# Transposing a unit's probabilities four steps behind its scores in place of three

## What is computed

```python
def hybrid_mixer(x, positions, w_in, conv_w, rel_bias, w_out):
    proj = jnp.einsum('bsd,dp->bsp', x, w_in)
    (cb, cc, ch, dq, dk, dv, iq, ik, iw, cq, ck, cv) = jnp.split(proj, offs, axis=-1)
    y_conv = short_conv_mixer(cb, cc, ch, conv_w)
    y_dsa = dsa_attention(dq, dk, dv, iq, ik, iw)
    y_chk = chunk_band_attention(cq, ck, cv, rel_bias)
    return jnp.einsum('bsm,md->bsd', jnp.concatenate([y_conv, y_dsa, y_chk], axis=-1), w_out)

def one_block(args):                                   # of dsa_attention
    logits = jnp.einsum('bqhd,bsd->bqhs', iqb, ik)
    score = jnp.einsum('bqh,bqhs->bqs', iwb, jax.nn.relu(logits))
    _, idx = lax.top_k(score, topk)                    # 128 keys of at most 512
    s = jnp.einsum('bqhd,bqkd->bhqk', qb, k_sel) * scale
    p = jax.nn.softmax(s, axis=-1)
    return jnp.einsum('bhqk,bqkd->bqhd', p, v_sel)
```

## Time and profile before

| | us |
|---|---|
| median of 3 executions | 2910.43 (2909.35 to 2912.76) |
| the profiled execution | 2910.82 |
| its span, first to last instruction | 2909.0 |
| PE busy | 2803.4 |
| DVE busy | 1659.9 |
| ACT busy | 1264.3 |
| POOL busy | 420.5 |

### The profile page before, as it was taken

How to read it: one execution, slowest core, us unless ns; L and a number is a source line. 1 busy time by engine, 2 the same in 40 slices (tenths; PEclk the granted TensorE clock), 3 DMA queues, 4 the chain that set the end, 5 groups by cost and what they waited for, 6 DMA issues and landing times.

```text
span 2909.0 us, 39181 instructions
## 1 busy us (share of the span) xinstructions
PE 2803.4 (96%) x15778; PEld 2360.8 (81%) x15782; DVE 1659.9 (57%) x2517; ACT 1264.3 (43%) x2157; POOL 420.5 (14%) x337
## 2 busy tenths in 40 slices
PE   8999999999989999999999999999999999999997
PEld 7878999998877788887668878888776688788886
DVE  5786545454776745445875466333659754563335
ACT  5574322234574422224554545333445535453333
POOL 2221000001222000001343120000313431200003
PEclk9999999999999999999999999999999999999999
DMA  4111232322112333232123213323221232233332
GB/s 143 50 44 66 88 95 83 96 91 80 52 44 66 98 99 95 97 98 84 52 76 113 87 66 95 99 94 98 84 80 55 71 111 88 72 95 94 95 98 69
DMA packets 71923, 244.36 MB, mean 84 GB/s; under 512 B 9152, under 2 KB 10816, under 8 KB 71744
## 3 DMA queue, kind: packets, MB, share of 16 engines
q1 hardware_dynamic: 66528, 235.50, 25.1%
q10 hardware_dynamic: 5216, 6.36, 0.7%
HBM read 239.73 MB, written 2.10 MB: 83 GB/s over the span
## 4 chain that ended last, share of the span: by engine, by line
PE 83%; DVE 11%; ACT 2%; issue 2%; POOL 1%; DMA 0%; ACTq 0%; DVEq 0%
PE psum L574 23%; PE psum L580 23%; PE psum L577 23%; PE psum L643 2%; DVE temp L2162 2%; DVE small L2160 1%; PE psum L669 1%; PE psum L675 1%; PE psum L671 1%; DVE weights_hi_lo L1723 1%; PE psum L1065 1%; PE psum L1077 1%; PE psum L762 1%; PE psum L904 1%; DVE small L2133 1%
## 5 line engine op out<-in xcount | busy, mean ns | idle before, releaser
L574 PE MATMUL psum<-act_hi_lo,weights_hi_lo 128*128 128x264 f32 (+2 forms) x2544 | 776.3, 344 | 3.6 <-ACT temp L1267 2.8
L577 PE MATMUL psum<-act_hi_lo,weights_hi_lo 128*128 128x264 f32 (+2 forms) x2544 | 752.5, 335 | 1.9 <-DVE weights_hi_lo L1723 1.9
L580 PE MATMUL psum<-act_hi_lo,weights_hi_lo 128*128 128x264 f32 (+2 forms) x2544 | 752.4, 335 | 0.0
L1160 ACT ACTIVATE weights_hi_lo<-weights_float 128x1024 fp32r<-128x1024 f32 (+2 forms) x446 | 463.6, 1042 | 524.6 <-PE psum L580 455.3
L1723 DVE TENSOR_TENSOR weights_hi_lo<-weights_float,weights_hi_lo 128x1024 fp32r<-128x1024 f32 (+2 forms) x446 | 555.4, 1246 | 224.1 <-ACT weights_hi_lo L1160 223.1
L574 PE MATMUL psum<-hidden_hi_lo,weights_hi_lo 128*128 128x512 f32 (+2 forms) x1584 | 520.7, 358 | 7.8 <-ACT arena L1503 4.8
L580 PE MATMUL psum<-hidden_hi_lo,weights_hi_lo 128*128 128x512 f32 (+2 forms) x1584 | 512.7, 353 | 2.3 <-POOL hidden_hi_lo L1986 2.2
L577 PE MATMUL psum<-hidden_hi_lo,weights_hi_lo 128*128 128x512 f32 (+2 forms) x1584 | 511.5, 353 | 0.0
L574 PEld LDWEIGHTS psum<-act_hi_lo,weights_hi_lo 128*128 128x128 f32 x2544 | 440.0, 189 | 70.8 <-issue 17.7
L577 PEld LDWEIGHTS psum<-act_hi_lo,weights_hi_lo 128*128 128x128 f32 x2544 | 439.3, 189 | 48.5 <-issue 2.6
L580 PEld LDWEIGHTS psum<-act_hi_lo,weights_hi_lo 128*128 128x128 f32 x2544 | 438.9, 189 | 48.2
(11 more groups left out here) (277 smaller groups left out, 3320.7 us busy)
## 6 DMA issues: line engine op xcount, KB each, us to landing
weights_float<-in_w_ff SPq DMA_DIRECT2D x128, 512.0 KB, 3.6
weights_float<-in_w_gu SPq DMA_DIRECT2D x88, 512.0 KB, 3.6
weights_float<-in_w_in SPq DMA_DIRECT2D x70, 512.0 KB, 3.7
weights_float<-in_w_down SPq DMA_DIRECT2D x32, 448.0 KB, 3.3
weights_float<-in_w_out SPq DMA_DIRECT2D x16, 512.0 KB, 3.6
weights_float<-in_w_down SPq DMA_DIRECT2D x16, 512.0 KB, 3.5
weights_float<-in_w_mv SPq DMA_DIRECT2D x16, 512.0 KB, 3.2
weights_float<-in_w_mix SPq DMA_DIRECT2D x16, 512.0 KB, 3.3
```

Source lines behind the costliest of these rows:

```text
L574: e.matmul(slot[:, place:place + c1 - c0], w_hi[:, col], x_hi[:, c0:c1], start=first, stop=False)
L577: e.matmul(slot[:, place:place + c1 - c0], w_lo[:, col], x_hi[:, c0:c1], start=False, stop=False)
L580: mm = e.matmul(slot[:, place:place + c1 - c0], w_hi[:, col], x_lo[:, c0:c1], start=False, stop=final)
L1160: e.activation(K.parts(n)[0][:, 0:cols], K.staged(n)[:, 0:cols], ACT.Copy).then_inc(*K.did("hi", n))
```

## The change

The transposes of a unit move from step t+3 to t+4, the weighted sums from t+4 to t+5, and with them ACT's two copies; DVE's low half moves from t+5 to t+6. Scores, exponentials, sums of probabilities and POOL's scaling stay where they were. The numbers of instructions stay the same on every engine.

```diff
--- before.py
+++ after.py
@@ -912,16 +912,16 @@
                 B.emptied((4 + c,), ("exp2", l, u, c))
 
     def turn(s):
-        if s - 3 in UNIT_AT2:
-            u, kind, p, i = UNIT_AT2[s - 3]
+        if s - 4 in UNIT_AT2:
+            u, kind, p, i = UNIT_AT2[s - 4]
             for c in range(2):
                 B.clear(6 + c)
                 w.wait_ge(*done("scaled", l, u, c))
                 for j in range(i + 1):
                     mm = e.transpose(K.bank[6 + c][:, j * P:(j + 1) * P], K.probs2[u % 2][c][:, j * P:(j + 1) * P], ident)
                 mm.then_inc(*did("turned2", l, u, c))
-        if s - 4 in UNIT_AT2:
-            u, kind, p, i = UNIT_AT2[s - 4]
+        if s - 5 in UNIT_AT2:
+            u, kind, p, i = UNIT_AT2[s - 5]
             w.wait_ge(*done("tok", l, 3))
             for c in range(2):
                 w.wait_ge(*done("turned2_out", l, u, c))
@@ -2098,8 +2098,8 @@
     for p in range(4):
         split_lo(e, w, K, first + p + 3)
     for s in range(TOK_STEPS, STEPS2 + 2):
-        if s - 5 in UNIT_AT2:
-            u, kind, p, i = UNIT_AT2[s - 5]
+        if s - 6 in UNIT_AT2:
+            u, kind, p, i = UNIT_AT2[s - 6]
             mix_at = (5 if kind == "c" else 2) + p
             hi, lo = K.hid_chunk(mix_at, T2)
             here = slice(i * P, (i + 1) * P)
```

## The result

The changed kernel is slower, by little: a median of 2913.95 us (2911.01 to 2915.89, 22 runs) against 2909.28 (2905.94 to 2914.17, 22 runs), a ratio of 1.0015 with an interval of 1.0009 to 1.0021. That is 4.7 us the wrong way, where 1.7 us of gain were forecast. It is within the 0.2% that one measurement was said to tell apart; with 22 runs on each side it can be told.

The account below looks back on a forecast made before the run. PE bounds the whole program, but DVE paces two stretches of the mixer stages. Gains of 1.5 (layer 0) and 0.2 (layer 1), tail nil, sum to 1.7 us: 2908.8 us forecast against a median of 2910.43, range 2904 to 2914.

Parts of the forecast that it names:

- The ring: Mixer stages: L2109 frees banks for transposes, these precede scores, scores feed DVE's maximum; priced at 0.2 us a layer.
- the 1.30 of the clock: Layer 0, 1417 to 1421: PE's low clock after two waits costs 1.30 us, which the change would win back.
- DVE's stretch from 1378.4 to 1418.6 taken over as it was: Stretch where DVE is busy 38.57 of 40.20 us; its times were kept unchanged as the start of the worked steps.
- Step 1: Step 61: transposes no longer precede L945, so L2139 starts at 1418.6 and DVE's gaps of 3.39 and 2.09 close.
- Step 2: Step 65: weighted sums move behind scores 64, so the gain shrinks; L945 at 30.0 against 32.1 in layer 0.
- Step 3: Step 69: L2139 at 41.3, against 43.59 in layer 0 and 42.3 in layer 1; gains 2.3 and 1.0.
- Step 4: After step 69 DVE is full: 0.6 for one more L2109 pair, 0.2 a layer for waits; mask 1.5 and 0.2 earlier.
- The tail: After the mask PE bounds; reordered sums and transposes there come to nil, with both ends 1 us.
- Waits that give nothing: PE's other waits before L921, where DVE is full, vanish and come back before scores or for L2109: no gain.
- The rival: PE's waits are worth full length: 12.2 us and 1.30 of clock go, 2896.9 us; chance 0.05, half recovered 0.06.
- the ring that turns the sign: Six places a layer from step 59's unit on each cost 1.04: 10.8 us slower, 2921.2 us; chance 0.08.
- the ring costs a little and eats the gain: The same six places a layer cost 0.1 to 0.3 us each: 2909.5 to 2912.5 us; chance 0.25.

Follow-up runs that it names:

- lofree_after: The changed kernel with L2109 making the low half from the high half alone, so it reads no bank: 2910.49 us, ratio 1.0005 to before.
- two_units_pool: The kernel before with only the units of steps 57 and 59 on the longer lags, and POOL's L2525 ahead of L2518: 2907.88 us, ratio 0.9998.
- d_only: The changed kernel with only the twelve "d" units on the longer lags, the "c" units on the old ones: 2909.91 us, ratio 1.0003 to before.
- mid: The changed kernel with the transposes between the two chunks of their step, so a dense matmul follows them: 2923.91 us, ratio 1.0043 to before.
- the lofree runs: Kernel before, changed kernel, and changed kernel with POOL's L2525 ahead of L2518, each with L2109 reading no bank: 2906.88, 2910.49 and 2909.48 us.
- two_units: The kernel before with only the units of steps 57 and 59 on the longer lags: 2910.32 us, ratio 1.0004 to before.
- pool_first: The changed kernel with POOL's L2525 ahead of L2518 where both fall in one step: 2909.43 us, ratio 1.0003 to before.
- before_pool: The kernel before with POOL's L2525 ahead of L2518 where both fall in one step: 2909.32 us, ratio 0.9998.
- the first two lofree kernels: The kernel before and the changed kernel, each with L2109 making the low half from the high half alone: 2906.88 and 2910.49 us.

## Why the prediction was wrong

Times in the text of this section are shifted so that a layer's first scores stand at 1350.56, as in the kernel before.

Three terms of the sum failed. The ring stood at 0.2 for a layer and costs 1.44 for a stage; POOL's queue stood at nothing and costs 1.25; and the 1.30 of the clock was not gained. Step by step:

- **"Before 1378.4 ... nil": right.** Scores 47 start 26.40 after the first scores (1374.65 less 1348.25), 26.64 in before.
- **DVE's stretch from 1378.4 to 1418.6 taken over as it was: failed.** By T54 the ring already holds: T54 stands 1.85 for L2109, which in its new place follows a mask of 1.26, step 57's maximum and sine product and a split. Scores 59 start at 1413.78 (1411.47 shifted by 2.31) where layer 1 of before has them at 1410.72 (2214.14 less 803.42). All units ahead of T57 were priced at nothing here; the 22 units beside those of steps 57 and 59 cost 1.4 for a stage, the largest part of the error, and 1.35 of it is there by scores 62. Not all of it need be the ring: at scores 57, ahead of T54, after is 0.63 later than before (55.07 and 54.44 after the first scores), and lofree_after, without the ring, is 0.66 later (55.10).
- **Step 1, the gap before L2139 near 1418.6 closes: right in mechanism, late in size.** L945 was forecast at 1417.4; two_units_pool has it at 1418.03, and after at 1419.46, since scores 59 are late. The sine product starts at 1420.52 against the forecast 1418.6 and 1420.65 in layer 1 of before, so after the change almost nothing is left of it.
- **Step 2, the chain to T59: right but for a queue left out.** T59's end of waiting was forecast at 1425.5; two_units_pool gives 1425.47 (1423.79 and 1.68). In after it is 1428.07. The forecast followed DVE, PE and ACT through steps 61 to 63 and never POOL: L2525 behind L2518 ends at 1422.29, and L2120 waits 1.17 for it. Before, the sine product was so late that POOL was always done. It costs 1.25 for a stage and stood at nothing in the sum.
- **Step 3: the gain at step 69 was forecast at 1.0 in layer 1: too high.** two_units_pool has its sine product 0.22 earlier in the layer at full clock, after has it 2.05 later.
- **The clock, 1.30 of the 1.7: not gained.** The low stretch did leave its place in layer 0, but the profile of after has one in layer 1 (2230), as before had one in layer 0. The mean granted clock of the 22 executions is 0.9936; executions of before taken beside the experiments have means of 0.9941 to 0.9944. A rise that the sum needed isn't there.
- **Step 4, the ring at 0.2 for a layer: mis-sized.** It measures 2.41 after against 0.97 before, 1.44 more. It is not where the step put it (T69 and later, which d_only shows free) but among the "c" units, with the largest waits at T54 and T59. The argument that arrivals lie within 0.3 of each other doesn't hold either: T69, T74 and T79 stand 0.45, 1.27 and 0.99 in after, though that costs nothing in d_only.
- **The signs.** No wait of L921 on L2518 is left, and the clock from 1417 to 1421 is 1.00, as named. DVE still stands 0.47 before L2139. The mask is 1.24 later in layer 0 (142.17 against 140.93) where 1.5 earlier was forecast: that is the sign that the step from 1378.4 on failed. The sign named for the ring, L2133 waiting again and again between 1443 and 1491, did not show, since the ring cost where the prediction had not looked.
- **The tail: nil, right.** From scores 89 to the end of the stage it takes 44.49 in after and 44.60 in before (1490.42 to 1534.91; 1491.49 to 1536.09). In PE's order of time the waits for the mask and for L1489 stay, and the 0.92 before T94 shrinks:

```profile
1490.42 1.13 PE L904 MATMUL psum<-arena 64*128 64x512 f32 x4 [1.17 <-DVE select_masks L2165]
...
1501.68 0.47 PE L669 MATMUL psum<-weights_hi_lo,act_hi_lo 128*128 128x512 f32 x1 [1.40 <-ACT act_hi_lo L1489]
...
1516.58 1.06 PE L921 MATMUL psum<-consts,temp 128*128 128x128 f32 x8 [0.35 <-DVE hidden_hi_lo L2109]
```

- **Waits that give nothing: right.** 12.2 us of waiting for POOL went and the time rose. PE's idle time in a stage hardly moved (184.19 less 170.10 is 14.1; 186.66 less 172.84 is 13.8) while the stage grew. The Trainium skill (Perfetto Trace Analysis, Identifying the Most-Contended Engine) would have the engine of highest occupancy optimized first, but judges TensorE by its rate of useful work and the busy share of its weight loads, not by that of its matmuls. The trace agrees where it is read for this stage and in that way: in layer 1 of before the weight loads are busy 114.67 of 184.19 (62%), DVE 148.43 (81%). The matmuls' 170.10 (92%) would name PE. The rival had left this condition out.

Of the rivals, the ring that turns the sign had the right mechanism with the wrong places and a price too high (1.04 at six places); "the ring costs a little and eats the gain" comes nearest, and 2913.95 lies just inside the range of 2904 to 2914, at its slow end. The sum by measured parts, for a stage: ring +1.44, and +1.03 for the rest, of which the queue is 0.96 (shown at one low stretch); together 2.47 by their making. Twice that is 4.9 against the measured 4.7. The forecast's own last step has a slip of 0.1: 1.7 below 2910.43 is 2908.7, not 2908.8.

**Left open.** Which of the ten "c" units beside those of steps 57 and 59 carries the 1.4 was not tried; scores 62 place it ahead of step 62, and T54's wait is the largest seen, but only as a row. The hand-over was not isolated by any run: mid moves it, and the lofree runs lengthen L2109. How much of the 1.41 that the 22 units cost is ring and how much hand-over stays open.

## What to carry to other kernels

When a hand-off between engines is moved one step, write down every resource that the moved work holds, and ask for each who takes it next and what stands ahead of the instruction that frees it; here T, which asks for banks 6 and 7, came to stand right before the scores, and the L2109 that frees them behind a mask. Close an idle spot on paper only after walking all engines that feed the next instruction, the slow ones too: a queue that was hidden by the old lateness (1.17 here) comes out as soon as the lateness goes. And move only the units that gain: moving two of 24, with POOL's order changed, gave the only gain of a stage seen here (0.22, too small for the median to show).

## What the hardware did that I had not expected

Transposes directly ahead of scores take PE longer than ahead of a dense matmul. PE in order of time, kernel before, where dense matmuls follow (start to start 0.64 for six, 0.36 for four):

```profile
2169.91 0.88 PE L921 MATMUL psum<-consts,temp 128*128 128x128 f32 x6
2170.55 0.48 PE L574 MATMUL psum<-act_hi_lo,weights_hi_lo 128*128 128x512 f32 x1
...
2177.26 0.60 PE L921 MATMUL psum<-consts,temp 128*128 128x128 f32 x4
2177.62 0.48 PE L574 MATMUL psum<-act_hi_lo,weights_hi_lo 128*128 128x512 f32 x1
```

And after, where scores follow (0.75 and 0.58):

```profile
1365.72 0.82 PE L921 MATMUL psum<-consts,temp 128*128 128x128 f32 x6
1366.47 0.49 PE L904 MATMUL psum<-arena 64*128 64x128 f32 x4
...
1374.07 0.66 PE L921 MATMUL psum<-consts,temp 128*128 128x128 f32 x4
1374.65 1.13 PE L904 MATMUL psum<-arena 64*128 64x512 f32 x4
```

That is 0.11 and 0.22 more. It happens at 21 places of a stage and makes most of PE's additional busy time (172.84 against 170.10): counted from start to start without the waits, L921 has 13.6 us of a stage in before and 16.4 in after. What it costs the stage no run isolates.

DVE's L2109 took longer in the lofree runs, where it reads its two operands outside the banks. Of its 96 executions in lofree_after ten took longer than 0.32 us, up to 1.31, each while POOL was at work; the other 86 took 0.27 to 0.29. In after, where one operand is in a bank, none took over 0.30, with POOL at work or not.

A low-clock stretch can cost nothing: two_units has a stage of 185.25 in both layers, at a clock of 1.00 and of 0.99, though PE was 1.56 longer busy in the second. There it makes scores 62 0.76 later and scores 64 only 0.01, since DVE waits 1.16 for POOL between them anyway; with POOL's order changed (two_units_pool) one costs 0.78. In before, after, pool_first, before_pool and the first two lofree kernels one cost 1.28 to 1.57.
